# First projection before the norm's root, and a new order of the first loads, in a mixer and mixture-of-experts layer

## What is computed

```
h    = rms_norm(x, norm_mix_g)                       # x * rsqrt(mean(x^2) + eps) * g
proj = h @ w_in                                      # 3840 columns
a_val, a_gate, u, g_conv, g_ssm = split(proj)
y_conv = silu(layer_norm(conv31(a_val * sigmoid(a_gate)) + conv_b)) @ w_conv_out
y_ssm  = s5_branch(u, ...) @ w_ssm_out               # 16 groups, 64 complex states, linear recurrence
x = x + (sigmoid(g_conv) * y_conv + sigmoid(g_ssm) * y_ssm) @ w_out
x = x + moe(rms_norm(x, norm_ffn_g))                 # top 4 of 32 experts, swiglu, 12 MB of weights each
out = rms_norm(x, norm_final_g)
```

## Time and profile before

| what | value |
|---|---|
| time, median of 3 runs | 1098.02 us (1097.78 to 1098.28) |
| profiled execution, span | 1098.9 us |
| TensorE busy, share of the span | 1055.4 us, 96% |
| VectorE, ScalarE, GpSimd busy | 298.8, 148.6, 81.1 us |
| moved by DMA | 431.52 MB, mean 393 GB/s |
| chain that ended last | TensorE 70%, DMA 26% |

### The profile page before, as it was taken

One profiled execution on the slowest core, in us unless ns is written; L12 is line 12 of the kernel. 1 busy time (PEld: TensorE's weight loads), 2 busy tenths in 40 slices (PEclk: granted clock), 3 DMA queues, 4 the chain that ended last, 5 costly groups with the idle time before them and its releaser, 6 DMA issues.

```text
span 1098.9 us, 12123 instructions
## 1 busy us (share of the span) xinstructions
PE 1055.4 (96%) x4955; PEld 452.5 (41%) x4956; DVE 298.8 (27%) x682; ACT 148.6 (14%) x267; POOL 81.1 (7%) x157
## 2 busy tenths in 40 slices
PE   7999999899999999999999999999999999989996
PEld 6888875333333333333333333333332333333332
DVE  5999842312111111111111111111111111111112
ACT  3011503111010101111010000000000000000003
POOL 2986100000000000000000000000000000000000
PEclk9999999999999999999999999999999999999999
DMA  8947796699999999999999999999999999999995
GB/s 243 269 141 281 316 357 253 255 429 426 429 437 430 429 435 428 433 433 428 437 431 429 434 427 431 433 429 435 429 432 435 428 432 433 431 432 425 427 422 240
DMA packets 43657, 431.52 MB, mean 393 GB/s; under 512 B 6775, under 2 KB 22445, under 8 KB 25484
## 3 DMA queue, kind: packets, MB, share of 16 engines
q1 hardware_dynamic: 43356, 430.60, 93.9%
q10 hardware_dynamic: 272, 0.52, 0.1%
HBM read 430.06 MB, written 1.05 MB: 392 GB/s over the span
## 4 chain that ended last, share of the span: by engine, by line
PE 70%; DMA 26%; ACT 1%; DVE 1%; another core or an unknown queue 1%; issue 0%; SPq 0%; DVEq 0%
PE bank L1550 30%; DMA ring<-w_gate_up 22%; PE bank L1562 14%; PE bank L1317 10%; PE bank L1576 4%; PE bank L1509 4%; DMA ring<-w_down 3%; PE bank L1452 3%; PE bank L1424 2%; ACT area L753 1%; PE bank L1516 1%; PE bank L1541 1%; PE bank L1521 1%; PE bank L1412 1%; DMA ring<-w_in 1%
## 5 line engine op out<-in xcount | busy, mean ns | idle before, releaser
L1550 PE MATMUL bank<-ring,area 128*64 128x512 f32 x2048 | 454.4, 600 | 20.0 <-DMA ring<-w_gate_up 19.8
L1550 PEld LDWEIGHTS bank<-ring,area 128*64 128x64 f32 x2048 | 148.8, 138 | 308.2 <-issue 270.6
L1562 PE MATMUL bank<-ring,area 128*64 128x512 f32 x1024 | 227.3, 595 | 5.5 <-ACT area L753 2.8
L1147 DVE TENSOR_SCALAR area<-bank 128x512 f32<-128x512 f32 x32 | 22.1, 692 | 671.3 <-PE bank L1550 671.3
L1562 PEld LDWEIGHTS bank<-ring,area 128*64 128x64 f32 x1024 | 71.7, 137 | 140.8 <-issue 132.5
L1317 PE MATMUL bank<-area,ring 128*128 128x256 f32 x480 | 107.8, 385 | 1.8 <-DMA ring<-w_in 1.8
L1317 PEld LDWEIGHTS bank<-area,ring 128*128 128x128 f32 x480 | 91.7, 192 | 16.2 <-DMA ring<-w_in 2.0
L759 ACT ACTIVATE area<-area 128x512 f32<-128x512 f32 x32 | 20.1, 630 | 487.8 <-DVE area L1147 487.8
L965 DVE SCALAR_TENSOR_TENSOR bank<-ring,spread,bank 128x256 f32<-128x256 f32 x174 | 71.5, 482 | 0.6
L1509 PE MATMUL bank<-rows,pick 128*64 128x512 f32 x256 | 63.6, 618 | 0.4 <-DVE onehot L1130 0.4
L1576 PE MATMUL bank<-area,spT 64*128 64x512 f32 x248 | 61.6, 615 | 0.7 <-ACT area L756 0.7
(11 more groups left out here) (254 smaller groups left out, 485.0 us busy)
## 6 DMA issues: line engine op xcount, KB each, us to landing
ring<-w_gate_up SPq DMA_DIRECT2D x48, 4096.0 KB, 46.8
ring<-w_down SPq DMA_DIRECT2D x25, 4096.0 KB, 44.3
ring<-w_gate_up SPq DMA_DIRECT2D x19, 2048.0 KB, 18.7
ring<-w_gate_up SPq DMA_DIRECT2D x26, 1024.0 KB, 9.2
ring<-w_down SPq DMA_DIRECT2D x18, 1024.0 KB, 12.5
ring<-w_in SPq DMA_DIRECT2D x15, 1024.0 KB, 8.1
ring<-w_down SPq DMA_DIRECT2D x5, 2048.0 KB, 12.7
ring<-w_conv_out SPq DMA_DIRECT2D x1, 3072.0 KB, 12.6
```

The source lines that it names most:

```text
L1147: return v.tensor_scalar(gc, bank[4][:, :], 7.0, None, ALU.min)
L1550: last = mm(bank[4 + b][64 * h:64 * h + 64, :], heT[:, k % 4, k // 4 * 64:k // 4 * 64 + 64], fours(w, b, h), start=False, stop=(k == KD - 1))
L1562: last = mm(bank[b][64 * h:64 * h + 64, :], src[:, k % 4, k // 4 * 64:k // 4 * 64 + 64], w[:, k % 2, h * 512:h * 512 + 512], start=(k == 0 ...
```

## The change

The first half of projection 0 runs on `hraw`, x times the norm's weight g without the root; its result is multiplied by the root afterwards (VectorE, into sig_a), and the sigmoid is taken of that. For this g is loaded ahead, on its own, and transposed between the two halves of x. VectorE makes four of the eight pieces of hraw, ScalarE the other four, from PSUM; hT is then hraw times the spread root. Ten products on the identity (START_WARM) stand ahead of TensorE's first transposes. w_in's first chunk is loaded in two halves right behind x and g, chunks 2 to 5 ahead of the state space parameters, and the other nine parameter loads are issued by ScalarE. The tap transposes stand between the first half of projection 0 and that of projection 1. fr and fi are made on VectorE after the first ten taps, their products with B on POOL; POOL masks C and B between table levels 4 and 5; TensorE transposes both after projection 5. Projection 14's first half comes ahead of the mean, the 96-row part of the bias split behind the scaling by the conv's root. Some function tables of ScalarE are loaded ahead by small dummies. Expert 28's loads go by the loop's semaphores.

```diff
-END = {E - 4: (4, 4, 4), E - 3: (4, 2, 2, 2, 2),
-       E - 2: (2, 2, 2, 2, 1, 1, 1, 1), E - 1: (2, 2, 2, 1, 1, 1, 1, 1, 1)}
+END = {E - 3: (4, 2, 2, 2, 2), E - 2: (2, 2, 2, 2, 1, 1, 1, 1), E - 1: (2, 2, 2, 1, 1, 1, 1, 1, 1)}
+START_WARM = 10
...
@@ SP
-            sp.dma_start(log_steps, ssm_log_step[0].rearrange("(t g) -> t g", g=2)).then_inc(par_in, 16)
...
+            sp.dma_start(par_rows[0:8, :], norm_mix_g[0].rearrange("(k p) -> k p", p=128)).then_inc(x_in[1], 16)
...
-            load_win(0)
+            sp.dma_start(win0[:, 0:4, :], win0_v[:, 0:4, :]).then_inc(win_in[0], 16)
+            sp.dma_start(win0[:, 4:8, :], win0_v[:, 4:8, :]).then_inc(win0_late, 16)
             load_win(1)
             sp.dma_start(tap_rows, conv_w[0]).then_inc(tap_in, 16)
+            for c in range(2, WRING):
+                load_win(c)
...
-            refill_end(E - 4, 0, PER)
+            refill(E - 6, 0, MIDDLE)
...
@@ POOL
+            def raw_b():
+                pool.wait_ge(ssm_in, 32)
+                pool.wait_ge(dve_f, 1)
...
             for k in range(LEVELS):
+                if k == 5:
+                    raw_c()
+                    raw_b()
...
@@ ACT
+            act.dma_start(log_steps, ssm_log_step[0].rearrange("(t g) -> t g", g=2)).then_inc(par_in, 16)
...
+            act.wait_ge(raw_dve, 1)
+            for k in range(4, KD):
+                act.wait_ge(xT_pe, k // 2 + 2)
+                s.activation(hraw[:, k, :], bank[k // 2][:, k % 2 * T:k % 2 * T + T], ACT.Copy, scale=g_early[:, k:k + 1])\
+                    .then_inc(raw_act, 1)
             act.wait_ge(spread_pe, 1)
             s.activation(rstd_all, bank[6][:, 0:T], ACT.Copy).then_inc(rstd_sb, 1)
+            act.wait_ge(params_pe, 1)
+            s.activation(par[:, :], bank[7][:, 0:62], ACT.Copy).then_inc(params_sb, 1)
+            s.activation(neg_top, ident[:, 0:2], ACT.Sigmoid)
+            act.wait_ge(params_pe, 2)
+            s.activation(late[:, 62:62 + KC * W], bank[7][:, 62:62 + KC * W], ACT.Copy).then_inc(params_sb, 1)
+            act.wait_ge(z_half, 1)
+            s.activation(sig_a[:, 0, :], sig_a[:, 0, :], ACT.Sigmoid).then_inc(half_sig, 1)
             act.wait_ge(params_sb, 1)
             s.activation(dt8, p_ls, ACT.Exp).then_inc(act_dt, 1)
...
+            take(2)
+            take(4)
+            take(5)
             act.wait_ge(rawT_pe, 1)
             s.activation(cT, grid(bank[0][:, :], 2, 2, 128), ACT.Copy).then_inc(rawT_sb, 1)
             s.activation(c_neg, grid(bank[0][:, :], 2, 2, 128)[:, :, 0, :], ACT.Copy, scale=-1.0).then_inc(rawT_sb, 1)
-            take(2)
             act.wait_ge(rawT_pe, 2)
             s.activation(bT, grid(bank[1][:, :], 2, 2, 128), ACT.Copy).then_inc(rawT_sb, 1)
-            take(4)
-            take(5)
...
@@ DVE
+            raw_rows(0)
             dve.wait_ge(x_sq, TT)
             var_of_sum(D).then_inc(var_x, 1)
+            raw_rows(1)
...
             for k in range(KD):
-                v.scalar_tensor_tensor(hT[:, k, :], bank[k // 2][:, k % 2 * T:k % 2 * T + T], p_g[:, k:k + 1],
-                                       rstd_all, ALU.mult, ALU.mult).then_inc(hT_ready, 1)
+                if k >= 4:
+                    dve.wait_ge(raw_act, k - 3)
+                v.tensor_tensor(hT[:, k, :], hraw[:, k, :], rstd_all, ALU.mult).then_inc(hT_ready, 1)
+                if k == 3:
+                    dve.wait_ge(half_pe, 1)
+                    v.tensor_tensor(sig_a[:, 0, :], half_bank[0][0], rstd_all, ALU.mult).then_inc(z_half, 1)
...
-            taps_of(order[:scanning])
+            taps_of(order[:LEAD])
+            discretize()
+            taps_of(order[LEAD:scanning])
...
-            dve.wait_ge(bias_in, 48)
-            bias_part(96)
             dve.wait_ge(var_pe, 1)
...
+            dve.wait_ge(bias_in, 48)
+            bias_part(96)
             bias_part(64)
@@ PE
+            for _ in range(START_WARM):
+                mm(bank[6][:, 256:384], ident[:, :], ident[:, :], start=True, stop=True)
...
+            def first_half():
+
+                w = grid(at(0, CH), KD, 256)
+                for k in range(KD):
+                    if k == 0:
+                        pe.wait_ge(win_in[0], 16)
+                    if k == 4:
+                        pe.wait_ge(win0_late, 16)
+                    if k in (0, 2):
+                        pe.wait_ge(raw_dve, 2 + k // 2)
+                    if k >= 4:
+                        pe.wait_ge(raw_act, k - 3)
+                    last = mm(half_bank[0][0], w[:, k, 0:128], hraw[:, k, :], start=(k == 0), stop=(k == KD - 1))
+                    if k == 3:
+                        spread_rstd()
+                last.then_inc(half_pe, 1)
...
-            project(0, (0,))
-            project(1, (0,))
+            first_half()
             pe.wait_ge(tap_in, 16)
             pe.wait_ge(params_sb, 1)
             for k in range(KC):
                 last = tr(bank[7][:, 62 + k * W:62 + k * W + W], tap_rows[:, k * 128:k * 128 + 128], ident[0:W, 0:W])
             last.then_inc(params_pe, 1)
+            project(1, (0,))
             project(0, (1,))
             project(1, (1,))
-            pe.wait_ge(raw_ready, 1)
             pe.wait_ge(params_sb, 2)
-            raw_transpose(craw, 0)
             project(2)
             project(3)
+            project(4)
+            project(5)
+            pe.wait_ge(raw_ready, 1)
+            raw_transpose(craw, 0)
             pe.wait_ge(raw_ready, 2)
             raw_transpose(braw, 1)
-            project(4)
-            project(5)
+            freed(4)
             pe.wait_ge(rawT_sb, 3)
-            freed(4)
             bu_pair(0)
...
+            project(14, (0,))
             pe.wait_ge(conv_done, KC + 1)
             pe.wait_ge(bu_sb, ST)
             mm(bank[0][:, 0:T], ones, conv[:, KC - 1, :], start=True, stop=False)
             mm(bank[0][:, 0:T], ones, conv_sum, start=False, stop=True).then_inc(mean_pe, 1)
-            project(14, (0,))
```

More of the change, by code:

```diff
@@ L175, in build @@
         late = spread[:, :, :, :].rearrange("p t d s -> p (t d s)")
-        par = late[:, 0:54]
-        gain_k = late[:, 54:62]
+        par = late[:, 0:62]
+        gain_k = late[:, 24:32]
         taps = grid(late[:, 62:62 + KC * W], KC, W)
@@ L1281, in _ @@
             pe.wait_ge(consts, 1)
+            for _ in range(START_WARM):
+                mm(bank[6][:, 256:384], ident[:, :], ident[:, :], start=True, stop=True)
             for t in range(TT):
[L1283 removed]
+                pe.wait_ge(x_in[t], 16 * (t + 1))
+                if t == 1:
+                    tr(bank[7][:, 0:8], par_rows[0:8, :], ident[0:8, 0:8]).then_inc(xT_pe, 1)
                 for k in range(KD):
[L1285 to L1295 removed]
+                    last = tr(bank[k // 2][:, (k % 2) * T + t * 128:(k % 2) * T + t * 128 + 128],
+                              x_sb[:, t, k * 128:k * 128 + 128], ident[:, :])
+                    if t == 1 and k % 2:
+                        last.then_inc(xT_pe, 1)
             ACT_TAKES = {n: i + 1 for i, n in enumerate([0, 2, 4, 5] + list(range(7, NCH)))}
@@ L1314, in project @@
                     for k in range(KD):
-                        if n == 0 and m == 0:
+                        if n == 1 and m == 0:
                             pe.wait_ge(hT_ready, k + 1)
@@ L1320, in project, with spread_rstd @@
                     last.then_inc(win_pe, 1)
-                elif n < 2:
+                elif n == 1:
                     last.then_inc(half_pe, 1)
+            def first_half():
[13 more added lines that the diff above has]
+                last.then_inc(half_pe, 1)
+            def spread_rstd():
+                pe.wait_ge(ones_ready, 1)
+                for t in range(TT):
+                    pe.wait_ge(diag_ready, t + 1)
+                    last = mm(bank[6][:, t * 128:t * 128 + 128], ones, diag[:, t, :], start=True, stop=True)
+                last.then_inc(spread_pe, 1)
+                pe.wait_ge(par_in, 16 * 9)
+                pe.wait_ge(ls_rows, 1)
+                tr(bank[7][:, 0:62], par_rows[:, :], ident[0:62, 0:62]).then_inc(params_pe, 1)
             def raw_transpose(raw, b):
@@ L1688, in _ @@
                     expert(i * 2 + half, half, [i * 16 + n for n in later(half)])
-            for e in range(E - 4, E - 2):
-                expert(e, e % 2, e)
+            expert(E - 4, 0, [(E // 2 - 2) * 16 + n for n in later(0)])
+            expert(E - 3, 1, E - 3)
             gates_up(E - 2, 0, E - 2)
```

150 lines of the change are left out of this document (73 added, 77 removed).

## The result

The changed kernel takes 1105.18 us (median of 6 runs, 1104.11 to 1108.25), the kernel before 1098.51 beside it: ratio 1.0059, interval 1.0042 to 1.0075. It is slower by 6.7 us, where 2.8 were forecast and the range ended at 1102.6.

A forecast was written before the change was run, and what follows sets the result against it. The front, TensorE's chain, was taken to set when the bounding expert weight stream starts. Terms -0.8 + 1.76 + 1.2 + 0.6 = +2.8 us gave 1100.8 us; range 1095.6 to 1102.6, likeliest case 1098.6 to 1101.9.

The forecast's parts named there:

- earlier start, conv_w's wait: Up to the second half-projection: 3.9 us won by starting earlier, of which TensorE's wait for conv_w leaves -0.8 us.
- clock: TensorE after its idle 3 us before conv_w: granted clock falls to 0.50, costing +1.76 us (bounds 0 and 3.5).
- raw transposes: Behind projection 5: TensorE waits for ScalarE's copies before the state space input, +1.2 us (0.9 to 1.5).
- mean and bias: Layer norm to state space product: too little TensorE work left behind the mean, +0.6 us (0.3 to 0.9).
- What bounds the kernel: Expert weight stream bounds the end; the front, TensorE's chain, sets its start, each microsecond there moving the end about one.
- Earlier start: Kernel start: w_in right behind x, first half ending near 12 us, hT at 14.0; 3.9 us won without other waits.
- The wait that moves: Tap transposes between half-projections: TensorE idle from about 12 to 15.1 us (13.5 to 15.6) for conv_w, leaving -0.8 us.
- The rival that the clock stays up: TensorE's idle 3 us before conv_w: no clock price, same sum without 1.76, 1099.0 us; chance 0.20.
- the one that conv_w comes in time: Tap transposes: conv_w does not hold TensorE, landed by 12 us; -2.1 us, 1095.9 us; chance 0.20.
- VectorE: Taps and state space lanes: 1 to 2 us late, but TensorE is as late itself, so nothing is added.
- GpSimd's lateness, the third rival: Tables before the first scan: POOL becomes late, some 1103 us; chance 0.12 together with any other new wait.
- The end: Expert 28's loads keep their sizes and order under other semaphores: nothing added.

The follow-up runs named there:

- conv_split: Changed kernel with conv_w loaded in two loads, of 16 and 15 rows, in the same place on the queue: 1098.94 us, ratio 1.0004 to the kernel before.
- conv_alone: Changed kernel with SP waiting for conv_w before issuing the third to sixth w_in load: 1102.99 us, ratio 1.0045 to the kernel before.
- clock_kept: Changed kernel with 22 identity products on TensorE ahead of its wait for conv_w: 1102.58 us, ratio 1.0038 to the kernel before.
- late_taps: Changed kernel with conv_w's wait and the tap transposes moved behind two more half-projections on TensorE: 1103.69 us, ratio 1.0051 to the kernel before.
- combo: conv_split plus the edits of raw_early and p14_back: 1098.76 us, ratio 1.0002 to the kernel before.
- cover: conv_split plus raw_early's edit, and ScalarE taking the step's exponential ahead of the tap copy and sigmoid: 1098.88 us, ratio 0.9988 to the kernel before.
- raw_early: Changed kernel with masked C and B transposed and copied ahead of projection 5 instead of behind it: 1104.02 us, ratio 1.0046 to the kernel before.
- p14_back: Changed kernel with projection 14's first half back behind the mean: 1105.50 us, ratio 1.0055 to the kernel before.

## Why the prediction was wrong

The direction and the mechanism were right, one term was mis-sized: the landing of conv_w, forecast at 15.1 us and measured at 18.04. By its steps, measured at the conv output product:

| step | forecast | measured | from |
|---|---|---|---|
| earlier start, conv_w's wait | -0.8 | +2.2 | transposes at 18.08, not 15.1 |
| clock | +1.76 | +2.2 | 40.07 - 38.20, and 0.84 - 0.5 in the transposes |
| raw transposes | +1.2 | +1.14 | 61.01 - 58.99 - 0.88 |
| mean and bias | +0.6 | +0.36 | 17.39 - 17.03 |
| sum | +2.8 | +5.9 | 142.69 - 136.80 = 5.9 |

*What bounds the kernel* held: 6 us at the conv output product are 6.7 in the time, and conv_split gives 6.76 there and 6.2 in the time.

*Earlier start* held to within a microsecond: the first half ended at 12.95 (forecast: near 12), hT at 14.75 (14.0).

*The wait that moves* is the step that failed: "Two w_in loads (2.10 MB) at 346 GB/s end 6.1 us after x's bytes, at 10.9; plus 3.8 gives 14.7". Every part was short. conv_w's first packet ran at 12.09, 1.2 us after 10.9 (11.30 to 12.11 in the six profiles with the same loads ahead of it): w_in's bytes do not begin at full rate when x's end. The DMA's rate in the first 30 us, in 40 slices of 0.75 us, shows it, first the change, then the kernel before:

```profile
GB/s 0 0 109 350 366 404 184 153 282 377 356 370 355 356 352 348 354 350 333 321 328 324 318 240 111 117 266 385 386 348 337 366 356 280 79 36 63 64 16 49
...
GB/s 0 0 115 366 415 426 103 11 83 223 382 384 367 350 350 344 318 107 29 103 28 21 9 97 244 367 390 349 281 313 360 352 351 348 354 352 354 344 347 348
```

Between 4.5 and 6.75 us (the seventh to ninth number) it is 184, 153 and 282; x's last packet is through at 5.75, where the kernel before had 4.89, and w_in's first runs at 4.85. The kernel before has the slow start too: its first w_in packet runs at 6.10, and the rate from 6.0 is 83, 223 and then 382. And 3.8 us for conv_w was read where its engine had nothing else to do, with a share of a sixteenth. The change puts four 1 MB loads right behind it, and it took 5.1 (conv_alone: 3.8). Last, from its last packet (17.21) to the release it took 0.8 us, where 0.4 were forecast. The upper bound of 15.6 had half a microsecond for a slow start, where 1.2 were needed, and nothing for the loads behind. The Trainium skill (DMA: Bandwidth & Descriptors, "Why a DMA increments its semaphore by 16 and not by 1") was cited for the one engine of 31 rows; conv_split agrees with it: cut into 16 and 15 rows, the same bytes are there at 13.42, and the trace has 31 arrivals on conv_w's semaphore instead of one.

*The clock* was right in kind and nearly in size, the size in part by luck: after the same kind of wait it was 1.7 to 2.9 us in other runs (last section). The advice of the Trainium skill (TensorE: Matmul & The Clock Gate, "Why this matters for your kernels") to warm the engine with matmuls first did not make the price 0 here: the ten products stood, and after 5 idle us the granted clock was 0.50. The Trainium skill gives that advice there for benchmarks; that it reaches across an idle stretch was the prediction's reading. Products inside the wait (clock_kept) kept it at 1.00. The rival that the clock stays up fell with it; so did the one that conv_w comes in time.

*The raw transposes* and *the mean* were right within their bounds.

*VectorE* was right only by its condition. The first tap came at 25.00 (20 to 21.5 forecast), the second lane's gated_half at 32.85 (28.2 to 29.3), the last states at 120.89, 2.5 us ahead of the second quad; "nothing is added" held because TensorE "is itself late by as much". late_taps and combo show what comes when it is not. GpSimd's lateness, the third rival, was the same lateness: it began with the sines at 23.85, its first rotation was done at 72.4, and TensorE did not wait for it in the change (in late_taps it did).

*The end* cost nothing that shows: conv_split keeps it and stands with the kernel before, though its front is 0.7 us earlier, so that a cost of a microsecond is not excluded. The remaining 0.6 to 0.8 us between front and time lie within the scatter of the expert stream; that they are only scatter was not shown.

The range failed for one reason: it treated the wait's length as known to a microsecond. The slow start could be read in the kernel before; the 3.8 us came from rows with no load behind conv_w.

## What to carry to other kernels

Cost a transfer that becomes a wait by the traffic of its new place, by what is queued behind it as much as by what is ahead of it, and spread small loads over the engines before something waits for them (conv_split: two lines, 6.2 us). When a wait is moved on one engine, ask what the other engines start from it: late_taps freed TensorE and gained 0.5 us at the conv output product, conv_split freed VectorE as well and gained 6.8. When a gain vanishes, look for the next engine that is late, and cover it with work that is ready (cover) before removing more.

## What was not expected of the hardware

The price of the fallen clock is not a constant. It was 1.87 us in the change, 2.94 in raw_early, 2.65 in p14_back (40.85 - 38.20) and 1.68 in conv_alone, after the same kind of wait: TensorE restarted at nearly the same time in all but conv_alone, but the stretch at 0.50 ended at another time in each (at 22.70 us the change shows 1.00 and raw_early still 0.50), and about half of what was left of it after the restart was lost: by the trace's clock records 4.6, 6.2 and 6.7 us were left in the change, p14_back and raw_early, and with the tap transposes 2.2, 3.0 and 3.3 us were lost. Differences of a microsecond between such kernels are therefore no verdict on their edits; the chain's pieces are.

A load on one engine was slowed by a third, from 3.8 to 5.1 us, by large loads queued behind it, although it was issued first; five profiles with these loads have 5.09 to 5.17 us.
